# Attention with its turns two jobs behind the scores and its projections spread to the last job, and outer products that take both banks first

## The chip, the cores and the metric

One core of a Trainium2 chip runs the whole kernel. The metric is the device time in microseconds of one execution; the time of the kernel before is the median of three runs. Five engines work side by side: PE (TensorE, matmuls), DVE (VectorE), ACT (ScalarE), POOL (GpSimd) and SP, which issues the weight transfers. Each runs its own instructions strictly in order, and they meet through semaphores.

## The reference, cut to what matters

Three residual blocks follow each other on a sequence of 512 tokens with 1024 features. The first mixes gated linear attention (GLA), a convolution and a spatial gating unit, then a feed-forward network. The second has two layers, each a half feed-forward network, an attention, and another half. The third mixes a linear recurrence (LRU) and an attention. The parts that the change touches:

```python
# second block, each layer: 8 "fox" heads and 4 "diff" heads of two parts, causal, S = 512
s_f = q_f @ k_f.T * scale + cum_q - cum_k          # fox, masked, softmax, then @ v_f
a_d = softmax(s_d[0]) - lam * softmax(s_d[1])      # diff, then @ v_d, then an rms norm
out = concat(o_f, o_d) @ w_out
# third block: 8 heads of 64; with 512 tokens and blocks of 256 all past keys are selected,
# so the kernel computes plain causal attention
y = concat(lru(xl) * silu(gl), attention(q, k, v) * silu(ga)) @ w_out
# first block, GLA in chunks of 64 tokens, forward and backward
s = decay * s + k_chunk.T @ v_chunk                # the outer product of a chunk
```

## The kernel before

Everything is fp32. A projection is computed as three matmuls per pair of 128x128 tiles (the weights and the activations are each split into a high and a low part): `products`, lines 1173 to 1175. The high parts of the weights are cast on ACT (`L1551`), the low parts subtracted on POOL (`L2615`). A projection tile of 1024 inputs is thus 24 matmuls of 512 columns; the attention takes it in two half units of 12 (`T_part`). A tile of `out` with 512 inputs is 12 matmuls.

The program is one Python text that every engine walks in the same order; each engine issues only its own instructions. The order of the text is therefore the order of every engine's queue. A semaphore wait is put in only where it isn't implied already.

`attend` (line 698) interleaves the attention with other work. `at.jobs` is a list of jobs (head, query block `qt` from 0 to 3); a job has `128 * (qt + 1)` keys. In the second block's layers jobs 0 to 15 are the four diff heads and jobs 16 to 31 the four pairs of fox heads; in the third block jobs 0 to 15 are four pairs of heads. A job goes through four steps:

- `scores`: PE multiplies two parts into two banks (`L1461`) and adds the mask (`L1464`); DVE takes the maximum of each (`L2470`, `L2472`); ACT takes the exponential and its sum, with a read of the accumulator (`L1842`), which frees the bank.
- `weigh`: DVE divides by the sum (`L2482`, `L2486`, `L2488`).
- `turn`: PE transposes the weights in blocks of 128 (`L1474`); ACT copies the result to SBUF (`L1849`). The ring for these copies has two slots: a diff job uses one, a pair of heads two.
- `gather`: PE multiplies with the values (`L1488`), and frees the slots. After `qt == 3`, `head_out` takes the head to its place.

Beside these, the generator `beside` is advanced: each `next` issues one unit. In a layer the units are 8 half units of `dqk`, 16 of `fqk` (each tile ends in `fox_in` on DVE, `L2461` and `L2462`), one empty yield, two of `diff_parts` (four high parts on ACT, `L1618`, and low parts on DVE, `L2014`), and 8 tiles of `out` with an empty yield behind each. With every unit one step of `norms` for the finished diff heads goes along (root `L1589`, `L2073`; row `L1247`, `L1604`; scaling `L2518`, `L2520`). In the third block the units are 12 half units of `z` (with the rms norm of the heads: mean matmuls `L1513`, square root `L1919`, reciprocals `L2574`; and the LRU's scans `L2567`), 8 of `gl`, two with the silus and the LRU's output, one of `head_parts`, and 8 tiles of `out3`.

Written out for the third block, one iteration of the loop before is: weigh j-1, scores j, gather j-2, unit, turn j-1, unit. For the layers' jobs 16 to 31 it is: weigh j-1, scores j, gather j-5, unit, turn j-3, unit, since the loop enters from the longer lag of the diff jobs.

PSUM has 8 banks in one ring (`Slots`): a bank is taken in order of age, and taking one makes the engine wait until its last use is over. The output of the gathers holds one, an unfinished half unit another.

The GLA chain (`chain`, `outer`, lines 1362 and 1383) makes, for each of 4 heads and 7 chunk steps, one outer product forward and one backward. Each is a matmul with 64 rows; the two use different halves of the rows. Each takes a bank (and waits for it) right before its matmul.

Of the kernel before, what the change touches and what calls it, by code (L numbers as in the profile page):

```python
# [77 lines left out]
class Tally:  # L78


    def __init__(self):
        self.at, self.counting = ({}, True)
# [214 lines left out]
def ring(k, name, aps, since=()):  # L297
    if name not in k.rings:
        k.rings[name] = Slots(aps, since)
    return k.rings[name]  # L300
# [356 lines left out]
class Heads:  # L657


    def __init__(self, k, tag, order, P, since):  # L660
        self.k, self.tag, self.since = (k, tag, since)
        self.jobs = [(h, qt) for h in order for qt in range(4)]
        self.P, self.T = (ring(k, 'P ' + tag, P, since), ring(k, 'T ' + tag, k.tmp[0:2], since))
        self.N = ring(k, 'N ' + tag, k.tmp[3:], since) if tag != 'm' else None
        first = 1 if tag == 'm' else 0
        self.stats = ring(k, 'stats ' + tag, [k.sm[:, 8 * i:8 * i + 8] for i in range(first, first + 8)], since)
        self.out = 0

    def parts(self, h):

# [27 lines left out]
def attend(on, at, beside):  # L698

    scored = weighed = turned = gathered = 0  # L700
    total = len(at.jobs)
    pair = lambda j: at.jobs[j][0][0] != 'd'
    while gathered < total:
        if scored < total and pair(scored):
            if weighed < scored:
                on.weigh(at, *at.jobs[weighed])
                weighed += 1
            on.scores(at, *at.jobs[scored])
            scored += 1
        elif scored < total:  # L710
            on.scores(at, *at.jobs[scored])
            scored += 1
        if turned > gathered and (pair(gathered) or turned - gathered > 1 or scored == weighed == turned):
            h, qt = at.jobs[gathered]
            on.gather(at, h, qt)
            gathered += 1
            if qt == 3:
                on.head_out(at, h)
                at.out += 1
        if weighed < scored and (scored == total or scored - weighed > 1):  # L720
            on.weigh(at, *at.jobs[weighed])
            weighed += 1
        two = turned < total and pair(turned)
        if two:
            next(beside, None)
        if weighed > turned and (two or weighed - turned > 2 or scored == weighed):
            on.turn(at, *at.jobs[turned])
            turned += 1
        next(beside, None)
    for _ in beside:  # L730
        pass


def second(on, k, layer, before):
# [31 lines left out]
    at = Heads(k, L, [('d', i) for i in range(4)] + [('f', i) for i in range(4)], k.P2, [last, ('lambda', L), ('forgot', L)])  # L766
# [5 lines left out]
    def projections():  # L772

        turn = None
        for n in (2, 6, 3, 7):
            on.T_part(('dqk', L, n), 'dqk' + L, n, A, 0, 2)
            if turn is not None:
                on.rope(L, turn)
            yield
            on.T_part(('dqk', L, n), 'dqk' + L, n, A, 1, 2)  # L780
            on.diff_in(L, n, R, last)
            turn = n
            yield
        for n in (0, 4, 1, 5, 2, 6, 3, 7):
            on.T_part(('fqk', L, n), 'fqk' + L, n, A, 0, 2)
            if n == 0:
                on.rope(L, turn)
            yield
            on.T_part(('fqk', L, n), 'fqk' + L, n, A, 1, 2)
            on.fox_in(L, n, R, last)  # L790
            yield
        yield
        for i in range(4):
            on.diff_parts(at, i)
            if i % 2:
                yield
        for n in range(KT):
            on.T(('outd_' + L, n), 'out' + L, n, at.OA, kt=4, first=4)
            on.part(res, n, ('outd_' + L, n))
            yield  # L800
            yield

    def norms():
# [8 lines left out]
    def both():  # L812
        one, two = (projections(), norms())
        while next(one, 'end') != 'end':
            next(two, None)
            yield
    attend(on, at, both())
    for n in range(KT):
        on.T(('out2_' + L, n), 'out' + L, n, at.OA, kt=4)
# [14 lines left out]
def third(on, k, res):  # L834
# [46 lines left out]
    def projections():  # L881
# [42 lines left out]
        for n in range(KT):  # L924
            on.T(('outl', n), 'out3', n, at.OA, kt=4)
            on.part(out, n, ('outl', n))
            yield
        on.head_parts(at, 2)
    attend(on, at, projections())
    on.head_parts(at, 3)  # L930
    for n in range(KT):
# [189 lines left out]
class Tensor(Engine):  # L1121
# [225 lines left out]
    def chain_begin(self, h):  # L1347
        for v in range(2):
            self.take(self.k.banks, 'bo', h, v, hold=True)
        for d in range(2):  # L1350
            self.outer(h, 0, d)

    def intra(self, h):
        k, e = (self.k, self.e)
# [6 lines left out]

    def chain(self, h, step):
        k, e = (self.k, self.e)
        for d in range(2 if step < 6 else 0):
            self.outer(h, step + 1, d)
        for d in range(2):
            c = step if d == 0 else 7 - step
            at = slice(64 * c, 64 * c + 64)
            if step == 0:
                state = k.SIN[:, d, h, :]  # L1370
                self.wait_ge('copied state', d, h)
            else:
                state = gla_ring(k).of(('st', h, d))[:, 256 * ((step - 1) % 2):256 * ((step - 1) % 2) + 256]
                self.wait_ge('state', h, d, step - 1)
            for v in range(2):
                m = e.matmul(self.bank('bo', h, v)[:, at], state[:, v * 128:v * 128 + 128], k.QE[:, d, at], start=step == 0 and d == 0, stop=step == 7 and d == 1, skip_group_check=True)  # L1376
            m.then_inc(*k.filled.inc(('inter', h, d, step), *([('free', ('st', h, d))] if step == 7 else []), *([('filled', ('bo', h))] if step == 7 and d == 1 else [])))
# [2 lines left out]
        for v in range(2):  # L1380
            self.k.banks.let(('bo', h, v))

    def outer(self, h, step, d):
        k, e = (self.k, self.e)
        c = step if d == 0 else 7 - step
        p, w = (64 * (c % 2), 256 * (h % 2))
        b = self.take(k.banks, 'kv', h, step, d)
        self.wait_ge('kd', h, d)
        self.wait_ge('value', h // 2, c // 2)
        e.matmul(b[:, 0:256], k.KD[p:p + 64, d, c // 2, :], k.VT[p:p + 64, c // 2, w:w + 256], start=True, stop=True).then_inc(*k.filled.inc(('filled', ('kv', h, step, d))))  # L1390

    def head_scale(self, s, h):
        sq = head_sum(self.k, h)
# [570 lines left out]
def gla_ring(k):  # L1964
    return ring(k, 'gla', k.tmp, [('normed', 'nx', 7)])
# [822 lines left out]
```

## Time and profile before

| | us |
|---|---|
| median of three runs | 3550.41 (3546.18 to 3551.94) |
| the profiled execution | 3547.52 |
| its span, first to last instruction | 3545.5 |
| PE busy | 3452.7 (97%) |
| DVE, ACT, POOL busy | 1244.3, 1260.8, 1522.3 |
| mean granted clock of PE | 0.988 of full speed |

The busy time of PE counts matmuls whose ends are modelled and overlap, so the table says that PE is hardly ever idle, not that it is at its peak. A wait of PE shows as idle time before an instruction with the engine that released it. Three stretches hold the attentions: 1702.8 to 1878.5 and 2709.5 to 2885 (the two layers) and 3375 to 3520 (third block). The GLA chain runs from 200 to 401.

### The profile page before, as it was taken

Reading aid. Unit: us, or ns where it says so; the run is one execution under the profiler, and the core shown is the slowest. Engines: PE = TensorE matmul, PEld = TensorE weight load, DVE = VectorE, ACT = ScalarE, POOL = GpSimd, SP = SyncE. Lnnn points to the kernel's source line nnn. Section 1 sums busy time; section 2 is a strip of 40 time slices with the busy share of each in tenths; the row PEclk is TensorE's granted clock in tenths of the full one; section 3 lists DMA queues with packets and bytes.
Section 4 is the critical chain, followed back from the end, with each engine's and each line's share of the span. In section 5 each row is a group of like instructions: output and inputs, shape, how many; then the busy total and the mean of one; then the engine's idle time right before and its main releaser. Section 6 shows DMA issues by size and latency. Waiting matters only on the chain.

```text
span 3545.5 us, 39140 instructions
## 1 busy us (share of the span) xinstructions
PE 3452.7 (97%) x16100; PEld 2776.8 (78%) x16100; DVE 1244.3 (35%) x2103; ACT 1260.8 (36%) x1926; POOL 1522.3 (43%) x709
## 2 busy tenths in 40 slices
PE   7999999998999999999999999999999999999988
PEld 3777887887888888887777888888887778887766
DVE  3165684531221135211553111111114652111574
ACT  4433323432322332223454222322233543222464
POOL 2422344655444444445424444444445234444333
PEclk8999999999999999999999999999999999999999
DMA  6211132442233323433112233232332022233211
GB/s 231 95 54 54 60 119 99 163 148 83 107 131 126 100 89 131 146 94 105 60 33 92 96 98 92 92 105 95 92 95 92 28 75 96 100 90 107 72 42 60
DMA packets 98717, 341.17 MB, mean 96 GB/s; under 512 B 11307, under 2 KB 11563, under 8 KB 98124
## 3 DMA queue, kind: packets, MB, share of 16 engines
q1 hardware_dynamic: 97632, 334.02, 28.3%
q10 hardware_dynamic: 908, 4.67, 0.3%
q8 instruction: 127, 2.08, 0.2%
q14 instruction: 50, 0.41, 0.0%
HBM read 336.02 MB, written 2.10 MB: 95 GB/s over the span
## 4 chain that ended last, share of the span: by engine, by line
PE 90%; DVE 4%; ACT 3%; POOL 1%; issue 1%; DMA 1%; ACTq 0%; DVEq 0%
PE ps L1173 25%; PE ps L1175 25%; PE ps L1174 25%; PE ps L1192 2%; PE ps L1461 2%; PE ps L1193 2%; PE ps L1194 2%; PE ps L1488 1%; PE ps L1474 1%; PE ps L1376 1%; DVE t L2574 1%; POOL t L2615 1%; PE ps L1247 1%; DVE t L2111 1%; PE ps L1229 0%
## 5 line engine op out<-in xcount | busy, mean ns | idle before, releaser
L2615 POOL TENSOR_TENSOR t<-t,t 128x1024 fp32r<-128x1024 f32 (+2 forms) x588 | 1362.8, 2320 | 1796.5 <-ACT t L1551 1795.4
L1173 PE MATMUL ps<-t,t 128*128 128x512 f32 (+1 forms) x4048 | 1607.5, 397 | 21.9 <-POOL t L2615 13.2
L1175 PE MATMUL ps<-t,t 128*128 128x512 f32 (+1 forms) x4048 | 1584.7, 391 | 0.0
L1174 PE MATMUL ps<-t,t 128*128 128x512 f32 (+1 forms) x4048 | 1580.4, 390 | 0.0
L1173 PEld LDWEIGHTS ps<-t,t 128*128 128x128 f32 x4048 | 764.5, 189 | 188.8 <-issue 16.7
L1175 PEld LDWEIGHTS ps<-t,t 128*128 128x128 f32 x4048 | 763.5, 189 | 167.7
L1174 PEld LDWEIGHTS ps<-t,t 128*128 128x128 f32 x4048 | 764.2, 189 | 157.7 <-issue 1.0
L1551 ACT CAST t<-t 128x1024 fp32r<-128x1024 f32 (+2 forms) x588 | 584.1, 995 | 568.4 <-PE ps L1175 423.6
L2414 DVE TENSOR_TENSOR t<-t,ps 128x512 f32<-128x512 f32 x110 | 75.7, 688 | 532.2 <-PE ps L1175 516.4
L1618 ACT CAST t<-t 128x512 fp32r<-128x512 f32 x158 | 97.0, 621 | 403.5 <-DVE t L2414 359.0
L1805 ACT ACTIVATE t<-t 128x512 f32<-128x512 f32 x88 | 55.6, 632 | 318.0 <-DVE t L2407 318.0
L2014 DVE TENSOR_TENSOR t<-t,t 128x512 fp32r<-128x512 f32 x138 | 119.9, 873 | 119.8 <-ACT t L1618 119.8
L2249 DVE SCALAR_TENSOR_TENSOR ps<-t,t,ps 128x392 f32<-128x392 f32 (+14 forms) x232 | 159.0, 685 | 6.2
L2375 DVE TENSOR_TENSOR t<-ps,t 128x512 f32<-128x512 f32 x32 | 22.1, 692 | 392.5 <-PE ps L1175 392.5
L2407 DVE TENSOR_TENSOR t<-ps,t 128x512 f32<-128x512 f32 x88 | 60.7, 690 | 250.9 <-PE ps L1175 225.0
L1192 PE MATMUL ps<-t,t 128*128 128x512 f32 x336 | 138.2, 411 | 10.6 <-POOL t L2615 7.6
L1842 ACT ACTIVATE t<-ps,t 128x128 f32<-128x128 f32 (+3 forms) x160 | 83.8, 528 | 165.8 <-DVE t L2472 99.5
L1194 PE MATMUL ps<-t,t 128*128 128x512 f32 x336 | 134.1, 399 | 0.0
L1193 PE MATMUL ps<-t,t 128*128 128x512 f32 x336 | 133.9, 399 | 0.0
L2629 POOL TENSOR_TENSOR t<-t,t 128x512 f32<-128x512 f32 x41 | 55.1, 1344 | 129.9 <-ACT t L1582 105.8
L2470 DVE TENSOR_REDUCE t<-ps 128x1 f32<-128x128 f32 (+3 forms) x160 | 77.5, 485 | 57.3 <-PE ps L1464 56.2
L1787 ACT ACTIVATE t<-t,t 128x512 fp32r<-128x512 f32 x48 | 34.7, 723 | 156.3 <-DVE t L2377 107.5
(278 smaller groups left out, 2374.9 us busy)
## 6 DMA issues: line engine op xcount, KB each, us to landing
t<-in_w_f1i SPq DMA_DIRECT2D x88, 512.0 KB, 3.3
t<-in_w_f2i SPq DMA_DIRECT2D x88, 512.0 KB, 3.2
t<-in_w_ada SPq DMA_DIRECT2D x72, 512.0 KB, 4.2
t<-in_w_ffi SPq DMA_DIRECT2D x44, 512.0 KB, 3.6
t<-in_w_f1o SPq DMA_DIRECT2D x32, 512.0 KB, 3.5
t<-in_w_f2o SPq DMA_DIRECT2D x32, 512.0 KB, 3.5
t<-in_w_gate SPq DMA_DIRECT2D x24, 512.0 KB, 4.0
t<-in_w_out SPq DMA_DIRECT2D x48, 256.0 KB, 2.6
```

The lines of the kernel that those rows point to most:

```text
L1173: e.matmul(out, wh[:, at], X.hi[c][:, 0:N], start=c == first, stop=False)
L1174: e.matmul(out, wh[:, at], X.lo[c][:, 0:N], start=False, stop=False)
L1175: m = e.matmul(out, wl[:, at], X.hi[c][:, 0:N], start=False, stop=c == final)
L1192: e.matmul(out, X.hi[c][:, at], wh[:, w], start=c == 0, stop=False)
L1193: e.matmul(out, X.hi[c][:, at], wl[:, w], start=False, stop=False)
L1194: m = e.matmul(out, X.lo[c][:, at], wh[:, w], start=False, stop=c == 7)
L1551: e.copy(k.WH[:, n % NHL, 0:w], k.raw[:, j % NRAW, 0:w]).then_inc(*k.rounded.inc(('rounded', j)))
L1618: e.copy(A.hi[t], src).then_inc(*k.act.inc(('hi', A.tag, t)))
L1842: e.activation(p[:, 0:n], self.bank('s', *key)[:, 0:n], ACT.Exp, scale=0.125, bias=st[:, 1:2], accum_out=st[:, 2:3]).then_inc(*k.act.inc(( ...
L2014: e.tensor_tensor(A.lo[t], src, f(A.hi[t]), ALU.subtract).then_inc(*k.dve.inc(('lo', A.tag, t), *events))
L2249: e.scalar_tensor_tensor((c3 if j == 30 else a3)[:, :, lo:hi], h3[:, :, lo + w - 15:hi + w - 15], param(k, 'conv_w', w * 8 + i), a3[:, :, ...
L2615: e.tensor_tensor(k.WL[:, n % NHL, 0:w], k.raw[:, j % NRAW, 0:w], f(k.WH[:, n % NHL, 0:w]), ALU.subtract).then_inc(*k.rest.inc(('rest', j) ...
```

## The change

`attend` is rewritten. `two` now follows the job to be scored, not the one to be turned. In that mode a job is turned when a further one has been weighed behind it (two behind its scores), every job that is turned is gathered in the next iteration, and the number of units per iteration is a rate: 1.0 in the layers, 1.9 in the third block, 2.0 once all is scored. The empty yield behind each tile of `out` goes. In the GLA chain `outers` takes both banks, with all waits, and then issues both matmuls.

```diff
-        self.out = 0
+        self.out, self.rate = (0, 1.9 if tag == 'm' else 1.0)
...
-    total = len(at.jobs)
+    total, due = (len(at.jobs), 0.0)
     pair = lambda j: at.jobs[j][0][0] != 'd'
     while gathered < total:
-        if scored < total and pair(scored):
-            if weighed < scored:
-                on.weigh(at, *at.jobs[weighed])
-                weighed += 1
+        two = scored == total or pair(scored)
+        if two and weighed < scored:
+            on.weigh(at, *at.jobs[weighed])
+            weighed += 1
+        if scored < total:
             on.scores(at, *at.jobs[scored])
             scored += 1
-        elif scored < total:
-            on.scores(at, *at.jobs[scored])
-            scored += 1
-        if turned > gathered and (pair(gathered) or turned - gathered > 1 or scored == weighed == turned):
+        ready = turned if two else turned - 1
+        while gathered < ready:
             h, qt = at.jobs[gathered]
             on.gather(at, h, qt)
             gathered += 1
...
-        if weighed < scored and (scored == total or scored - weighed > 1):
+        if not two and scored - weighed > 1:
             on.weigh(at, *at.jobs[weighed])
             weighed += 1
-        two = turned < total and pair(turned)
         if two:
-            next(beside, None)
-        if weighed > turned and (two or weighed - turned > 2 or scored == weighed):
+            due += at.rate if scored < total else 2.0
+            if due >= 1.0:
+                due -= 1.0
+                next(beside, None)
+        while turned < weighed - (2 if not two else 1 if scored < total else 0):
             on.turn(at, *at.jobs[turned])
             turned += 1
-        next(beside, None)
+        while due >= 1.0 or not two:
+            due -= 1.0 if two else 0.0
+            next(beside, None)
+            if not two:
+                break
...
             on.T(('outd_' + L, n), 'out' + L, n, at.OA, kt=4, first=4)
             on.part(res, n, ('outd_' + L, n))
             yield
-            yield
...
-        for d in range(2):
-            self.outer(h, 0, d)
+        self.outers(h, 0)
...
-        for d in range(2 if step < 6 else 0):
-            self.outer(h, step + 1, d)
+        if step < 6:
+            self.outers(h, step + 1)
...
-    def outer(self, h, step, d):
...
+    def outers(self, h, step):
+        k, e, w = (self.k, self.e, 256 * (h % 2))
+        both = []
+        for d in range(2):
+            c = step if d == 0 else 7 - step
+            both.append((d, c, self.take(k.banks, 'kv', h, step, d)))
+            self.wait_ge('kd', h, d)
+            self.wait_ge('value', h // 2, c // 2)
+        for d, c, b in both:
+            p = 64 * (c % 2)
+            e.matmul(b[:, 0:256], k.KD[p:p + 64, d, c // 2, :], k.VT[p:p + 64, c // 2, w:w + 256], start=True, stop=True)...
```

## Rows read from the trace of the kernel before

**Rows 1.** The page's part 4: the chain of waits, by engine.
```profile
PE 90%; DVE 4%; ACT 3%; POOL 1%; issue 1%; DMA 1%; ACTq 0%; DVEq 0%
```

**Rows 2.** Waits of PE, whole span: line, releaser, us in total, times, longest.
```profile
PE ps L1488 <- ACT t L1849: 11.3, 7, 5.1
PE ps L1474 <- DVE t L2488: 8.6, 4, 3.7
```

**Rows 3.** Windows: length, busy of PE, PEld, DVE, ACT, POOL, clock, DMA share, GB/s.
```profile
1702.80:1878.50 175.70, 171.13 (x1010) 129.08 (x1010) 107.68 (x323) 89.31 (x229) 47.65 (x28) 1.00 0.12 40
...
3375.00:3520.00 145.00, 127.03 (x686) 91.21 (x684) 92.74 (x177) 82.17 (x172) 45.13 (x25) 0.95 0.13 42
```

**Rows 4.** Windows of PE alone, third block: length, PE busy, clock, DMA share, GB/s.
```profile
3405.00:3410.00 5.00, 2.62 (x12) 1.00 0.14 58
3410.00:3417.00 7.00, 5.66 (x17) 0.51 0.01 4
...
3478.30:3485.00 6.70, 5.62 (x22) 0.50 0.00 0
```

**Rows 5.** Timeline of PE, first layer: start, us, instruction, idle before and releaser.
```profile
1815.90 1.13 PE L1247 MATMUL ps<-t,t 128*128 128x128 f32 x8 [0.22 <-DVE t L2482]
...
1819.03 1.53 PE L1461 MATMUL ps<-t,t 80*128 80x384 f32 x4 [1.34 <-ACT t L1842]
...
1825.36 0.47 PE L1173 MATMUL ps<-t,t 128*128 128x512 f32 x1 [0.44 <-DVE t L2014]
...
1870.46 1.09 PE L1488 MATMUL ps<-t,t 128*64 128x128 f32 x16 [0.90 <-ACT t L1849]
...
1877.26 1.09 PE L1488 MATMUL ps<-t,t 128*64 128x128 f32 x16 [1.25 <-ACT t L1849]
```

**Rows 6.** Timeline of PE, third block.
```profile
3383.88 0.70 PE L1461 MATMUL ps<-t 64*128 64x256 f32 x4 [2.40 <-DVE t L2584]
...
3390.29 0.44 PE L1474 MATMUL ps<-t,t 128*128 128x128 f32 x2 [2.66 <-DVE t L2488]
...
3411.34 1.54 PE L1474 MATMUL ps<-t,t 128*128 128x128 f32 x6 [3.73 <-DVE t L2488]
...
3478.46 1.12 PE L1488 MATMUL ps<-t,t 128*64 128x128 f32 x8 [5.07 <-ACT t L1849]
...
3519.01 1.09 PE L1488 MATMUL ps<-t,t 128*64 128x128 f32 x16 [1.15 <-ACT t L1849]
```

**Rows 7.** Timeline of ACT and DVE, first layer.
```profile
1815.25 0.27 ACT L1589 ACTIVATE t<-ps,t 128x8 f32<-128x8 f32 x1
...
1829.62 0.69 ACT L1842 ACTIVATE t<-ps,t 128x512 f32<-128x512 f32 x1 [2.55 <-DVE t L2472]
...
1817.38 0.67 DVE L2461 TENSOR_TENSOR t<-ps,t 64x512 f32<-64x512 f32 x1
...
1819.85 0.75 DVE L2518 SCALAR_TENSOR_TENSOR t<-t,t,t 128x512 f32<-128x512 f32 x1 [1.07 <-ACT t L1604]
...
1828.65 0.69 DVE L2470 TENSOR_REDUCE t<-ps 128x1 f32<-128x512 f32 x1
...
1831.69 0.48 DVE L2488 TENSOR_SCALAR t<-t,t 128x512 f32<-128x512 f32 x1
```

**Rows 8.** Timeline of ACT and DVE, third block.
```profile
3400.62 1.28 ACT L1919 ACT_TABLE_LOAD   x1
3401.91 1.26 ACT L1919 ACTIVATE t<-ps,t 128x512 f32<-128x512 f32 x2
3403.07 0.65 ACT L1849 COPY t<-ps 128x256 f32<-128x256 f32 x2
...
3412.11 0.69 ACT L1842 ACTIVATE t<-ps,t 128x512 f32<-128x512 f32 x1 [6.61 <-DVE t L2472]
...
3402.63 6.57 DVE L2574 RECIPROCAL t<-t 128x512 f32<-128x512 f32 x2 [3.68 <-ACT t L1919]
```

**Rows 9.** Timeline of PE, the later of two outer products that a wait parts.
```profile
264.98 0.70 PE L1390 MATMUL ps<-t,t 64*128 64x256 f32 x2 [1.15 <-DVE t L2218]
```

More of the change, by code:

```diff
@@ L1381, in chain_end @@
             self.k.banks.let(('bo', h, v))
-    def outer(self, h, step, d):
[L1384 to L1390, printed above, removed]
+    def outers(self, h, step):
[8 more added lines that the diff above has]
+            p = 64 * (c % 2)
+            e.matmul(b[:, 0:256], k.KD[p:p + 64, d, c // 2, :], k.VT[p:p + 64, c // 2, w:w + 256], start=True, stop=True).then_inc(*k.filled.inc(('filled', ('kv', h, step, d))))
     def head_scale(self, s, h):
```

## The prediction

> **What bounds the kernel now.** PE is busy 97% of the span by the table, and holds 90% of the chain of waits [rows 1]. The waits of PE come next: all of them are some 93 us (span less PE busy), and those at the attention's lines are small: 11.3 us of products with the values waiting for ACT's copies, 8.6 us of transposes waiting for the weighing on DVE [rows 2]. The windows then show where: the attention of a layer takes 175.7 us (the second 175.5) with 4.6 us of idle PE at full clock, that of the third block 145 us with 18 idle and a mean clock of 0.95 [rows 3]. So order alone can win some 27 us. The question is which wait ends last at each place, and what the clock does: in the third block it was at 1.2 GHz from 3410 to 3417 and from 3478 to 3485 (0.51 and 0.50), each time following an idle PE (3.73 and 5.07 us); after waits of 2.40 and 2.66 us it stayed at 2.4 [rows 4, 6].
>
> **The order before and after**, from the loop. A job is a pair of heads and one block of queries (128 to 512 keys in turn); a half unit is 12 matmuls of a projection, 2.9 us (12 of them in 2.62 us of a window [rows 4]). In the steady state of the third block an iteration j was: scores j, gather j-2, half unit, turn j-1, half unit. It becomes: scores j, gather j-3, half unit, turn j-2, mostly a half unit. In the layers' second half (jobs 16 to 31) the old order trailed further (gather j-5, turn j-3) and used two half units per iteration until the projections were gone; the new one is scores j, gather j-3, one half unit, turn j-2. Jobs 0 to 15 of the layers keep their order.
>
> **Layers: what goes.** The old waits near the end of the fqk projections are 0.22, 1.34, 0.44 and once more some 0.4 us, and in the tail 0.90 and 1.25 [rows 5]: 4.5 us, and 5.9 with what the starts of matmuls lie further apart there (1.4 us, read from the starts). The tail gets half units: turn 31 has one behind it, and its gather (1.25) is free. But jobs 29 and 30 are now turned and gathered in a row. The ring T has two slots, a pair takes both, so ACT copies job 30 only behind gather 29: 0.86 for two copies of 384 keys (an estimate; 0.65 for 256, 1.07 for 512, by the row of 256 [rows 8]) and 0.45 of hand-over, 1.3 us of wait. The tail thus falls from 3.0 to 1.3.
>
> **Layers: what comes.** (a) Turn j-2 is now followed at once by scores j+1 and its gather, where a half unit used to lie between. With 256 keys turned and 128 scored that is 1.1 us of PE against 1.33 (two copies 0.65 [rows 8] and the hand-over): 0.25 once or twice, the other sizes fit. (b) The norm of a diff head puts a root on ACT ahead of those copies: table 1.28 and root 0.27 [rows 7]. Heads 2 and 3 meet it now, turn 15 and turn 19: 1.55 + 0.54 or 1.07 of copies + 0.3 against 1.9 and 2.4 us of PE, 0.6 each, 1.2 in all. This replaces the 1.34 and the 0.22 above. (c) The largest: three yields hold no matmul (one empty, two of diff_parts). Before, two came in one iteration; now each takes an iteration, so PE meets four scores without a half unit, right behind the last fox_in. From its end, in DVE's order: fox_in 1.36 and the last norm step 1.1 to 2.5; weighing job 23 1.1 to 3.6; the maxima of job 24 0.85 to 4.45; ACT's two exponentials with their reads to 5.1, then the copies of job 22 (0.86) to 5.95 [rows 7], the sizes below 512 keys from the same stretch. PE has done turn 21, scores 24, gather 21, turn 22 and scores 25 by 3.4 and waits 2.6. The same walk gives 1.0 for job 23, 1.35 for job 24 (behind four high parts of 0.56 each on ACT, while their four low parts of 0.65 hold DVE) and 0.9 for job 25: 5.9 in all. Bounds: 1.5 us (DVE's own work of 10.9 us in those iterations against PE's 9.7, each summed from its instructions) and 9 us, if the clock falls once. I take 5.9, since every term has a row. Per layer 0.3 + 1.2 + 5.9 + 1.3 = 8.7 against 5.9: +2.8, for both +5.6.
>
> The Trainium skill (ScalarE: Activation LUTs, What ACT_TABLE_LOAD costs) adds 1.38 us of drain to a load of 1.28, 2.66 a switch; the rows show the activation right behind a load of 1.28 (3400.62 and 3401.91) [rows 8]. By its figure (an estimate) the two places of (b) would cost 1.4 us more each, +5.5 us over both layers; the sum goes by the row.
>
> **Third block.** (d) Iteration 0 has one half unit, not two (1.9 owed). Scores 1 need a bank of the value projection, which DVE empties just before 3383.88 whatever PE does; PE waited 2.40 for it and now, one half unit earlier at it, 5.2 [rows 6]. The half unit lies behind the scores and fills the 2.66 us of turn 0: the two cancel to +0.1. But a wait of 5.2 is as long as the one after which the clock was at half; half the 5.4 us that follow is 2.7, of which I count 2.3. (e) The head norms put two 128x512 reciprocals of 3.3 us on DVE, three times (6.57 each time) [rows 8]. Before, turn 2 and turn 6 waited for the weighing behind them (3.73 [rows 6], 1.28), the second set hid. Turn 2 is one iteration later and free. But the reciprocals now come as the second half unit of iterations 2, 4 and 6, so the maxima, the exponentials of the next job and, behind these in ACT's order, the copies of the job before all queue behind them. From the end of the mean matmuls: reciprocals to 7.7 (sqrt behind a cast and a table load), weighing 1.0, maxima of 512 keys 1.6, second exponential 0.9 later, a copy of a projection 0.6, copies 0.65: 12.8. PE until gather 1: scores 1.28, gather 0.37, half unit, turn 0.36, half unit, scores 0.64: 8.5. Gather 1 waits 4.3 (perhaps as scores 4, whose bank the exponential holds); gather 3 has smaller jobs, 10.8 against 9.4, 1.4; gather 5 3.7. Sum 9.4 against 5.0. The first is again followed by a low clock with a good chance (2.5 before, 2.0 counted now). Bounds for (e): -5.0 and -2.5 of clock if the copies do not queue, +10 if each wait costs clock. (f) ACT's four silus and a table load stand ahead of the copies for gather 9 (5.07 before [rows 6], 8.4 us from the last gl half unit to the gather). Job 11 has 512 keys where job 10 had 384, 0.9 later, with 0.6 less of PE before it: 6.6. Turn 10 no longer waits 0.92. +0.6. (g) In iteration 9 turn 7 has nothing behind it, 0.3. Tail: gather 14 behind gather 13 on one ring 1.3, gather 15 1.3, for 0.77 and 1.15 before [rows 6]: +0.7. Sum (d) to (g): 0.1 + 2.3 + 4.4 - 0.5 + 0.6 + 1.0 = +7.9.
>
> **Outer products.** Both waits now stand ahead of both matmuls. The Trainium skill (TensorEngine Tiling (Array Packing), Key Properties) says tiles on different rows run in parallel, which speaks for keeping them together; but only 3 of the 28 pairs are apart (as the one whose later matmul waits 1.15 for the state update) [rows 9]. In these the second starts when its bank is free either way, and the first (0.6) moves from before the wait to beside it: 0. Bounds -1.9 (three first matmuls on the path) and +1.9.
>
> **Sum.** +5.6 + 7.9 = +13.5 on the profiled 3547.5 gives 3561. That execution lies 2.9 below the median of the three runs (3546.2 to 3551.9); against the median it would be 3564. I take 3562. What a measurement of this kernel tells from no change is 0.2%, 7.1 us: faster is below 3543.3, slower above 3557.5.
>
> **Rivals.**
> A, faster (0.15): the copies keep up. One mechanism: with turns two behind, weighing never stops PE in the third block (2.66 + 3.73 + 1.28, 2.5 of clock), gathers 1, 3 and 5 find their copies made, and the tails win 1.7 twice. That is -10.2 - 3.4 = -13.6, 3537. For it: the 8.6 us of transposes are DVE's alone. Against: ACT runs in order, and its exponential waited 6.61 us for the maxima behind the reciprocals [rows 8]. It decides at 8.5 us from the mean matmuls to gather 1: if job 1's copies come sooner, A holds.
> B, no change (0.27): the old turn waits and new gather waits are of one size, and (c) is at its lower bound since PE's own work covers DVE: about +2, 3552.
> C, the clock (0.16): each of the new waits of 3 us and more (scores 1, gathers 1 and 5, the two layers' gather 22) is followed by a spell at 1.2 GHz that costs 2.5 to 3.4. Beyond what is counted that is 3 more, +9: 3571. Rows 4 speak for it, since both long waits had one; against it, the waits of 2.4 and 2.66 had none.
> The forecast's own case holds 0.42 (3554 to 3570). Slower over 0.2% is C and nearly all of it, 0.58; within 0.2% B and little else, 0.28; faster 0.14. The range takes in most of B and the near end of A, and reaches above C: 3542 to 3578.
>
> **What would show it.** In the changed profile: the 8.6 us of transposes waiting for the weighing nearly gone, and waits of gathers for copies up from 11.3 to over 25 us in all; scores 1 of the third block waiting over 5 us; after the last fqk unit three gathers or scores in a row that wait; gather 1 waiting over 3 us right behind the reciprocals; three or four spells at half clock in the third block instead of two; the tail with one wait of 1.3 per layer; the outer products' stretch unchanged within 2 us. I am wrong if gather 1 doesn't wait, or if the stretch of either layer comes out below 175 us.

## The result, and the profile after

The changed kernel takes 3559.55 us (median of 13 runs, 3555.91 to 3568.3) against 3550.37 of the kernel before in the same session (13 runs): ratio 1.0029 [1.0022, 1.0037]. That is 9.2 us slower by the medians and 8 to 13 by the interval. The prediction was 3562. The profiled execution took 3560.8 (span 3558.9), 13.3 more than that of before.

The windows of the profile after, stretch by stretch: the two layers' attention from first scores to last gather, the third block's, and the stretch of the outer products. Columns as in [rows 3].

```profile
1701.80:1882.90 181.10, 175.09 (x1009) 131.99 (x1008) 108.56 (x323) 90.57 (x228) 46.79 (x28) 0.97 0.11 37
2714.20:2894.10 179.90, 172.26 (x1010) 130.42 (x1009) 109.19 (x323) 90.25 (x228) 46.77 (x28) 0.99 0.12 38
3385.90:3533.40 147.50, 127.56 (x685) 92.31 (x684) 90.10 (x177) 81.80 (x171) 42.98 (x25) 0.93 0.13 42
...
199.10:404.20 205.10, 196.66 (x1107) 159.01 (x1106) 121.16 (x217) 67.53 (x89) 51.34 (x23) 0.97 0.15 52
```

The first layer's and the outer products' stretch in the kernel before, cut at the same points:

```profile
1702.80:1878.30 175.50, 170.93 (x1010) 128.88 (x1009) 107.68 (x323) 89.21 (x228) 47.65 (x28) 1.00 0.12 40
...
200.40:400.40 200.00, 195.31 (x1105) 156.52 (x1104) 121.15 (x217) 67.43 (x89) 51.47 (x23) 0.98 0.16 52
```

So the layers are longer by 5.6 and 4.4 us, the third block by 2.7 (144.8 before), the outer products by 5.1. The rest of the program gives 4.5 back in this pair of executions (4.8 between the outer products and the first layer, at places the diff doesn't touch). Idle PE is length less busy: 4.6 before in a layer, 6.0 and 7.6 after. The rest of the layers' loss is PE being busy longer at a lower clock (175.1 and 172.3 against 170.9). In the first layer most of it is one spell at half clock that begins in the wait of gather 22 (PE alone; length, busy, clock, DMA share, GB/s):

```profile
1832.20:1842.40 10.20, 9.64 (x46) 0.50 0.00 0
```

The waits of PE over the whole span after, answering to [rows 2] (L1495 gathers, L1856 ACT's copies, L1468 scores, L2591 DVE's copies of the value projection, L2489 the weighing, L1849 the exponentials, L1397 outer products, L2225 the state update):

```profile
PE ps L1495 <- ACT t L1856: 22.4, 16, 6.1
...
PE ps L1397 <- DVE t L2225: 5.5, 3, 1.9
...
PE ps L1468 <- DVE t L2591: 5.1, 1, 5.1
...
PE ps L1468 <- DVE t L2489: 2.9, 1, 2.9
...
PE ps L1468 <- ACT t L1849: 2.7, 4, 1.6
```

The 8.6 us of transposes waiting for the weighing are gone, as meant. Gathers went from 11.3 to 22.4, and scores from 5.1 (2.4 and 2.7 before) to 10.7 (5.1, 2.9 and 2.7). The timeline of PE shows where: the second layer first, then the third block.

```profile
2798.26 2.50 PE L1495 MATMUL ps<-t,t 128*128 128x128 f32 x10 [1.25 <-ACT t L1856]
2823.56 0.88 PE L1495 MATMUL ps<-t,t 128*64 128x128 f32 x12 [0.67 <-ACT t L1856]
2846.72 0.88 PE L1495 MATMUL ps<-t,t 128*64 128x128 f32 x12 [2.42 <-ACT t L1856]
2854.61 0.44 PE L1495 MATMUL ps<-t,t 128*64 128x128 f32 x4 [1.12 <-ACT t L1856]
2859.46 0.66 PE L1495 MATMUL ps<-t,t 128*64 128x128 f32 x8 [0.44 <-ACT t L1856]
2885.63 0.88 PE L1495 MATMUL ps<-t,t 128*64 128x128 f32 x12 [1.05 <-ACT t L1856]
...
3394.55 1.22 PE L1468 MATMUL ps<-t 64*128 64x256 f32 x4 [5.08 <-DVE t L2591]
3422.25 0.49 PE L1468 MATMUL ps<-t 64*128 64x128 f32 x4 [2.91 <-DVE t L2489]
3443.76 1.09 PE L1495 MATMUL ps<-t,t 128*64 128x128 f32 x16 [0.83 <-ACT t L1856]
3461.90 0.49 PE L1468 MATMUL ps<-t 64*128 64x128 f32 x4 [1.61 <-ACT t L1849]
3463.70 1.12 PE L1495 MATMUL ps<-t,t 128*64 128x128 f32 x8 [1.10 <-ACT t L1856]
3494.76 1.12 PE L1495 MATMUL ps<-t,t 128*64 128x128 f32 x8 [6.07 <-ACT t L1856]
3526.83 0.88 PE L1495 MATMUL ps<-t,t 128*64 128x128 f32 x12 [1.05 <-ACT t L1856]
3532.40 1.09 PE L1495 MATMUL ps<-t,t 128*64 128x128 f32 x16 [0.87 <-ACT t L1856]
```

In order these are gathers 13, 18, 22, 24, 25 and 30 of a layer, then scores 1, scores 4, gather 3, scores 8, gather 5, gather 9, and the two gathers of the tail. The first of them is the one that the prediction has no term for. ACT's timeline ahead of it shows what stands before the copies (2797.84): the exponentials of job 16, a copy, a cast and a square.

```profile
2795.19 0.37 ACT L1849 ACTIVATE t<-ps,t 128x128 f32<-128x128 f32 x1 [5.71 <-PE ps L1481]
...
2795.89 0.58 ACT L1864 COPY t<-ps 128x512 f32<-128x512 f32 x1
2796.36 1.06 ACT L1558 CAST t<-t 128x1024 fp32r<-128x1024 f32 x1
2797.30 0.64 ACT L1878 ACTIVATE t<-t 128x512 f32<-128x512 f32 x1
2797.84 0.76 ACT L1856 COPY t<-ps 128x256 f32<-128x256 f32 x2
```

### The profile page after: what moved, and what is told of

Its sections match the earlier page's. It is cut to its first block, busy times and chain, and to the rows that moved or that the text cites. A ratio compares the mean times of both kernels' runs of the same rounds, so it can differ in the third digit from the quotient of the medians.

```text
span 3558.9 us, 39103 instructions
## 1 busy us (share of the span) xinstructions
PE 3461.6 (97%) x16100; PEld 2786.9 (78%) x16100; DVE 1241.0 (35%) x2103; ACT 1263.0 (35%) x1926; POOL 1520.7 (43%) x709
## 4 chain that ended last, share of the span: by engine, by line
PE 91%; DVE 3%; ACT 3%; POOL 1%; issue 1%; DMA 1%; ACTq 0%; DVEq 0%
PE ps L1177 26%; PE ps L1179 25%; PE ps L1178 25%; PE ps L1196 2%; PE ps L1197 2%; PE ps L1198 2%; PE ps L1468 2%; PE ps L1495 1%; PE ps L1379 1%; PE ps L1481 1%; DVE t L2581 1%; PE ps L1251 1%; POOL t L2622 1%; DVE t L2118 1%; PE ps L1397 0%
## 5 line engine op out<-in xcount | busy, mean ns | idle before, releaser
L1177 PE MATMUL ps<-t,t 128*128 128x512 f32 (+1 forms) x4048 | 1610.0, 398 | 18.3 <-POOL t L2622 11.3
L1849 ACT ACTIVATE t<-ps,t 128x128 f32<-128x128 f32 (+3 forms) x160 | 84.3, 529 | 154.2 <-DVE t L2479 122.4
L2066 DVE SCALAR_TENSOR_TENSOR t<-t,t,t 128x1024 f32<-128x1024 f32 x49 | 80.9, 1651 | 33.6 <-DMA t<-in_w_ada 33.5
```

The costliest lines, as they stand in the source:

```text
L1177: e.matmul(out, wh[:, at], X.hi[c][:, 0:N], start=c == first, stop=False)
L1849: e.activation(p[:, 0:n], self.bank('s', *key)[:, 0:n], ACT.Exp, scale=0.125, bias=st[:, 1:2], accum_out=st[:, 2:3]).then_inc(*k.act.inc(( ...
```

## The experiments: the parts of the change

**One: the outer products alone**, in the kernel before.

```diff
-        for d in range(2):
-            self.outer(h, 0, d)
+        self.outers(h, 0)
```

> Only the outer products are changed; both attentions keep the order of before. My theory (the waits only move from between two matmuls to ahead of them): the stretch from the first to the last outer product stays 200 us but for spells of the lower clock, the three separated pairs show one wait of 1.8 us ahead of both instead of 1.1 between them, attentions at 175.4, 175.4 and 144.8, total within 2 us of before. Rival (the pairs gain by running side by side): 2 us less in that stretch. Rival (the state updates get late, which explains the 205 us seen with the whole change): 3 to 5 us more, in every run.

3547.44 us, ratio 0.9999 [0.9990, 1.0008] (3 rounds). The stretch took 200.3 against 200.0. The three separated pairs wait 1.86 us ahead of both matmuls, where before a matmul, a wait of 1.15 and the second matmul stood: the ends are the same. In this pair of profiles the edit costs 0.3 us.

**Two: the new loop in the layers alone; three: in the third block alone.** Both keep the new outer products; the other stage uses the old loop.

```diff
+def attend(on, at, beside):
+    (attend_new if at.tag != 'm' else attend_old)(on, at, beside)
```

> The new loop only in the two layers of the second block, the old one in the third block, outer products new. Theory: the layers carry most of the loss, since ACT's copies now stand between a turn and the gather two steps behind it: attention stretches of 180 to 181 and 180 us, 144.8 in the third block, total +8 to +10 against before. Rival (the loss is made in the third block, by scores 1 and the gathers behind the reciprocals): total within 3 us of before.

3551.67 us, 1.0009 [1.0001, 1.0018]. The layers took 179.4 and 179.3 us, the third block 144.5.

```profile
1702.30:1881.70 179.40, 172.17 (x1009) 130.36 (x1008) 109.32 (x323) 90.50 (x229) 46.84 (x28) 0.99 0.12 38
```

Idle PE is 7.2 us (4.6 before), busy PE 1.2 more: +3.9 per layer, of which 2.7 are waits and the rest goes with 3.4 us at half clock from gather 22 on. The two layers are thus 7.7 us longer in this profile, near what was expected, but the total moved by 3.2 (0.4 to 6.4) and not by 8 to 10; why the rest doesn't reach the total stays open.

> The new loop only in the third block, the old one in the layers, outer products new. Theory: turn waits are exchanged for gather waits of nearly the same size; stretch 147 to 148 us against 144.8, layers 175.4 each, total +2 to +4. Rival (what the prediction gave): +7.9 in that stretch.

3552.18 us, 1.0009 [1.0000, 1.0018]. Third stretch 148.1 (+3.3), with the same waits as in the changed kernel. The stretch is what the theory said, 147 to 148. The two parts alone sum to 6.4 us, the whole measures 9 to 10; with intervals of some 3 us on each part, the difference can't be called an interaction.

**Four: turns before the half unit**, that is, the changed kernel without the half unit between gathers and turns.

```diff
             due += at.rate if scored < total else 2.0
-            if due >= 1.0:
-                due -= 1.0
-                next(beside, None)
         while turned < weighed - (2 if not two else 1 if scored < total else 0):
```

> As the changed kernel, but the turn comes right behind the gather and all units behind the turn: a half unit then lies between a turn and the next gather, and ACT makes the copies ahead of the unit's casts and high parts. Theory (copies behind ACT's queue are what PE waits for in the layers): gather 13 no longer waits 1.25, nor gathers 15 and 18 to 21; gather 22 still waits about 2.4 as its copies stand behind an exponential that DVE holds up; layers at 176.5 to 178 us each, 3 to 4 less than with the change. In the third block the wait for the silus moves from gather 9 to the first tile of out3, 146 to 148. Total 6 to 8 us below the changed kernel. Rival (the loss comes from the lack of units in four iterations alone): layers still 179 or more.

3559.02 us, 1.0027 [1.0017, 1.0036]: no better than the change. The wait of gather 13 is gone, but those of gathers 22, 24 and 25 grew from 2.42, 0.85 and 0.46 (first layer of experiment two) to these, in the first layer:

```profile
1837.79 1.47 PE L1492 MATMUL ps<-t,t 128*64 128x128 f32 x12 [3.03 <-ACT t L1853]
1847.33 0.44 PE L1492 MATMUL ps<-t,t 128*64 128x128 f32 x4 [1.39 <-ACT t L1853]
1852.95 0.66 PE L1492 MATMUL ps<-t,t 128*64 128x128 f32 x8 [1.27 <-ACT t L1853]
```

A layer came to 178.9 and 179.0, 0.3 to 0.5 under experiment two and not the expected 176.5 to 178: the rival held. The third block came to 144.7, 2.8 under the changed kernel (gather 9 waits 1.55, the first tile of `out3` 3.8 for POOL), but the outer products' stretch was 206.8 in this profile. In the layers, what PE doesn't wait at one place it waits at the next that depends on the same queue.

## The experiments: what the waits hang on

**Five: half units spread.** The splits of the diff heads ride on fox half units, so that one empty iteration remains behind the last of these and one is put four later.

```diff
+            if n == 3:
+                on.diff_parts(at, 0)
+            if n == 7:
+                on.diff_parts(at, 1)
             yield
...
+            if n == 7:
+                on.diff_parts(at, 2)
             yield
+        on.diff_parts(at, 3)
         yield
-        for i in range(4):
-            on.diff_parts(at, i)
-            if i % 2:
-                yield
...
             yield
+            if n == 3:
+                yield
```

> The changed kernel, but the splits of the diff heads' tiles ride on half units of the last fox projections (head 0 with fqk 3, heads 1 and 2 with fqk 7), so that of the three yields without matmuls one is left for head 3, and one empty yield is put between the fourth and fifth tile of the output projection. The four scores in a row without a half unit become two single iterations, four apart. My theory (term c): the waits of that zone, 2.4, 0.2, 1.1 and 0.4 in the second layer, are owed to the missing half units in a row: they fall to 1.5 or less, each layer's stretch from 180 to 181 to 177 to 178, the total by 4 to 7. Rival (DVE's own work sets that zone, its 10.9 us against PE's 9.7): half of it stays wherever the half units lie; the stretch falls by 1 to 1.5 only. Second rival: the splits on ACT and DVE now stand ahead of the exponentials of jobs 20 and 22 and make waits of their own there; 180 stays.

3563.01 us, 1.0039 [1.0026, 1.0053]; layers 181.6 and 180.8. My theory fell for the first wait and held for those behind it: gathers 24 and 25 no longer wait, but gathers 18 and 22 (the two rows) wait 1.19 for 0.67 and 3.54 for 2.42, and gather 31 of the tail waits 0.87 where it was free. Idle PE is 8.5 us a layer, 1.3 more.

```profile
2826.33 0.88 PE L1500 MATMUL ps<-t,t 128*64 128x128 f32 x12 [1.19 <-ACT t L1861]
2850.59 0.88 PE L1500 MATMUL ps<-t,t 128*64 128x128 f32 x12 [3.54 <-ACT t L1861]
```

DVE's timeline tells why. Behind the last fox_in (L2473, L2474) now stands a low part of the split (L2026, 0.69), then the norm (L2530 and one more), the weighing, and only then the maxima for which ACT's exponential waits, with a high part of the split (0.61 on ACT) and the copies for gather 22 behind it:

```profile
2844.25 0.69 DVE L2474 TENSOR_TENSOR t<-ps,t 64x512 f32<-64x512 f32 x1
2844.98 0.69 DVE L2026 TENSOR_TENSOR t<-t,t 128x512 fp32r<-128x512 f32 x1
2845.59 0.75 DVE L2530 SCALAR_TENSOR_TENSOR t<-t,t,t 128x512 f32<-128x512 f32 x1
...
2847.81 0.29 DVE L2482 TENSOR_REDUCE t<-ps 128x1 f32<-128x128 f32 x1
```

0.69 + 0.61 = 1.3 us more in the queues, 1.1 more of wait. The walk of term (c) through the queues is thus right; that it needs four iterations without a half unit is not. The first wait hangs on what stands in DVE's queue behind the last half unit.

**Six and seven: no reciprocals.** The head norms' reciprocals of the third block work on 8 of 512 columns, in the changed kernel and in the kernel before (the rest of that norm is left out).

```diff
-            e.reciprocal(m, m).then_inc(*k.dve.inc(('head rstd', n)))
+            e.reciprocal(m[:, 0:8], m[:, 0:8]).then_inc(*k.dve.inc(('head rstd', n)))
```

> The changed kernel with the head norms' reciprocals on 8 of 512 columns only (the norms of the third block's queries and keys are thus left out for the others). My theory (term e): the two reciprocals of 3.3 us in a row are what scores 4 (2.9 us), gather 3 (0.8), scores 8 and gather 5 (1.6 and 1.1) wait for, through the maxima and the exponentials queued behind them. All of these go, and the spells at 1.2 GHz from 3423 to 3426 and 3464 with them: the third stretch falls from 147.5 to 137 to 140. Scores 1 keeps its 5 and gather 9 its 6. Rival (ACT's own load in those iterations, with two table loads): scores 4 and gather 5 still wait over 1.5 each, and the stretch stays above 142.

> The kernel before with the head norms' reciprocals on 8 of 512 columns only, as in the leave-out run of the changed kernel (the norms of the third block's queries and keys are left out for the others). It tells what the new order is worth when DVE is not behind. My theory: of the old waits turn 0 (2.66) and scores 1 (2.40) and gather 9 (5.1) stay, turn 2 (3.7), its spell (3.4 lost) and turn 6 (1.3) go: third stretch 144.8 to 136 to 137.5, above the changed kernel's 134.6 in the same leave-out, so that the order itself gains 1.5 to 3 there and it is the place of the reciprocals that turns this into a loss. Rival: the old order gains as much or more without them (134.6 or less), so that the new order loses by itself, through scores 1 and gather 9.

One execution of each, 3546.80 and 3541.53 us; third stretches, the changed order first:

```profile
3384.60:3519.20 134.60, 124.06 (x685) 89.92 (x685) 65.47 (x175) 79.89 (x167) 42.01 (x25) 0.96 0.14 46
```

```profile
3379.80:3514.00 134.20, 123.74 (x685) 89.37 (x684) 73.70 (x175) 79.75 (x167) 43.83 (x25) 0.97 0.14 46
```

Scores 4 and 8 and gathers 3 and 5 no longer wait; even scores 1 fall to 2.5, which I had expected to keep their 5 (in the changed kernel DVE's two reciprocals at 3369.54 stand ahead of the value copies, too). The rival, ACT's own load, fell with the waits. So the reciprocals cost 12.9 us in the new order and 10.6 in the old, and the difference, 2.3, is nearly the whole of the third block's 2.7, as far as one execution of each can tell. But my view that the new order gains 1.5 to 3 by itself fell: without reciprocals both take the same within 0.4. It is neither better nor worse there, it only takes the reciprocals at a worse place.

**Eight: two half units in iteration 0** of the third block, in the changed kernel.

```diff
-    total, due = (len(at.jobs), 0.0)
+    total, due = (len(at.jobs), 0.1 if at.tag == 'm' else 0.0)
```

> The changed kernel, but the third block starts with 0.1 owed, so that iteration 0 has both half units and iteration 1 one. My theory (term d): scores 1 wait for a bank that DVE empties at a fixed time; with one more half unit in front the wait falls from 5.1 to 2.3 as it was before, the spell at 1.2 GHz from 3392 (6.8 us, worth 3.4) no longer follows, and since turn 0 stays one iteration later, the 2.7 us that it cost before don't come back: third stretch 147.5 to 142 to 144.5, total 3 to 5 less. Rival: what PE saves at scores 1 it waits at scores 4, whose bank comes with the exponentials behind the reciprocals at a time of its own: 2.9 there becomes 5 to 6, and the stretch stays at 146 to 147.5.

3561.07 us, 1.0040 [1.0026, 1.0054]; third stretch 150.2, 2.7 longer where 3 to 5.5 less was expected. Scores 1 wait 2.40 again, and what follows waits instead:

```profile
3398.68 0.70 PE L1468 MATMUL ps<-t 64*128 64x256 f32 x4 [2.40 <-DVE t L2591]
3408.00 0.47 PE L1177 MATMUL ps<-t,t 128*128 128x512 f32 x1 [1.52 <-POOL t L2622]
3413.57 3.33 PE L1520 MATMUL ps<-t,t 128*128 128x512 f32 x4 [2.57 <-ACT t L1922]
3427.66 0.80 PE L1468 MATMUL ps<-t 64*128 64x128 f32 x4 [2.69 <-DVE t L2489]
```

The rival had this at scores 4; it is the mean matmuls (L1520) that wait, for ACT's squares. The 2.7 us saved at scores 1 came back as 4.1 (1.52 and 2.57) in other places than either theory named, and PE was busy 1.5 us longer.

## The experiments: can it be had faster

**Nine: heads split early.** In the kernel before, a pair's query norm comes one iteration ahead of its key norm, so that no two reciprocals follow each other.

```diff
-                    on.head(pair, half + 1)
                     on.head(pair + 4, half + 1)
...
             on.head_in(n, last)
+            on.head(n, 0)
             yield
...
                 on.T_part(('z', n + 4), 'z3', 12 + n, A, half, 2)
+                on.head(n, half + 1)
...
-            on.head(n, 0)
```

> The kernel before, but the query half of each pair's head norm (mean matmul, root, reciprocal, scaling) comes one iteration earlier than the key half, so that the reciprocals of 3.3 us stand alone instead of two in a row. My theory: it is the 6.6 us in a row that turn 2 (3.7 us, and the spell at 1.2 GHz after it) and turn 6 (1.3) wait for; with 3.3 at a time the slack of an iteration covers them: the third stretch falls from 144.8 to 137 to 140, the total by 5 to 8 below the kernel before. Rival: each root now has a table load of 1.28 and one back to the exponentials of its own on ACT, three pairs more; the copies and exponentials come later by 2.6 in each iteration and PE waits 1 to 1.5 at each of three more places: 142 to 146, total within 3 of before.

3550.24 us, 1.0007 [0.9998, 1.0016]; third stretch 149.9, 5 longer. The rival held, and more: the mean matmuls wait 2.70 for a square just issued, and ACT is busy 90.4 us in the stretch, 8 more, and gathers wait for its copies, up to 1.89.

**Ten: key reciprocals late.** Means, roots and table load stay together; only the second reciprocal and its scaling are issued one iteration later on DVE. **Eleven:** the same on the changed kernel.

```diff
-                    on.head(pair + 4, half + 1)
+                    on.head(pair + 4, 3 * half + 1)
...
+                if half == 0 and pair is not None:
+                    on.head(pair + 4, 3)
+                    on.head(pair + 4, 2)
...
-        if s == 1:
+        if s == (1 if n in (0, 1, 2, 3, 4) else 3):
```

> The kernel before, but in the third block the reciprocal of a pair's keys and its scaling are issued one iteration later than those of its queries; mean matmuls, roots and their table load stay together. Between the two reciprocals of 3.3 us now lie the weighing and the maxima of an iteration. My theory: turn 2 (3.7 us and the spell at 1.2 GHz behind it) and turn 6 (1.3) wait for two reciprocals in a row; with one of 3.3 the slack covers it, and there is no second table load as in the earlier split: the third stretch falls from 144.8 to 136 to 140, the total by 5 to 8. Rival: the scores of the next pair need the scaled keys, and DVE, which is now behind, is late with them: scores 4 wait 2 to 4 us instead, the stretch stays at 143 to 146.

> The same edit on the changed kernel. My theory: scores 4 (2.9) wait for a bank held by an exponential behind both reciprocals, as do scores 8 and gather 5 (1.6 and 1.1); with one reciprocal at a time these fall by 3.3 each to nothing, as far as the leave-out run showed (134.6): third stretch 147.5 to 138 to 142, scores 1 and gather 9 keep their 5 and 6; the total 6 to 9 below the changed kernel, 3550 to 3554, still above the kernel before with this edit by what scores 1, the layers and gather 9 cost. Rival: in this order a pair's scores follow the last half unit of its norm more closely (in iteration 4 only one half unit lies between), so scores 4 wait for the scaled keys: 145 to 147.

On the kernel before: 3546.36 us, 0.9994 [0.9985, 1.0003], third stretch 140.6, 4.3 shorter, between the theory's 136 to 140 and the rival's 143 to 146. On the changed one: 3556.93, 1.0032 [1.0021, 1.0044], third stretch 145.2, 2.3 shorter, as the rival had it; the total shows none of it. Turn 2 no longer waits 3.73, turn 6 not 1.28; scores 4 wait, as the rival said:

```profile
3418.28 0.49 PE L1466 MATMUL ps<-t 64*128 64x128 f32 x4 [2.74 <-DVE t L2566]
```

and on the changed kernel

```profile
3418.72 0.80 PE L1473 MATMUL ps<-t 64*128 64x128 f32 x4 [4.12 <-DVE t L2494]
```

(2.91 before this edit). In both, PE starts 0.15 us after DVE has scaled the pair's keys (the ends of that are 3418.13 and 3418.56); the rows name the instruction behind it. Scores 8, gathers 3 and 5 are free in both.

**Twelve: gates first.** As ten, with the gl projections ahead of those of the last pair, so that the silus ride on a half unit.

```diff
+        on.T_part(('z', 3), 'z3', 11, A, 0, 2)
         for n in range(4):
             on.lru_silu(n)
...
+        yield
```

> The kernel before with the late key reciprocals, and the gate projections (gl) put ahead of the last pair's query and key projections, so that the four silus ride on a half unit of the latter instead of standing with the splits behind the last half unit. My theory: gather 9's 5.1 us are copies queued behind four silus and their table load on ACT after the last half unit; with silus two iterations earlier, among half units, that wait falls under 2.5 and the spell at 1.2 GHz from 3478 goes: third stretch another 3 to 6 below the run with late reciprocals alone, 131 to 136 if that one is at 138. Rival: the wait follows the missing half units, not the silus: two yields without matmuls remain behind z 7 with the splits of the recurrence's tiles on ACT, and the gather there waits 4 to 5 again; only the place changes. Second rival: the silus delay the exponentials among the half units by 3.8 us and a turn there waits 2 or more instead.

3545.77 us, 0.9993 [0.9984, 1.0002]; third stretch 141.8 where 131 to 136 was expected. Gather 9's wait for copies falls from 5.07 to 2.50, and a wait of 2.00 for the split of the recurrence's tiles on POOL comes behind it, with the low clock behind both. The first rival, that the wait follows the missing half units, is borne out in part. Against ten nothing was won. Ten and twelve are the fastest measured of the kernels that leave nothing out, but neither is told from the kernel before by its interval.

## Why the prediction was right, and where it was not

The sign and the main mechanism held: turns no longer wait for the weighing, and gathers and scores wait longer for what stands in the queues of ACT and DVE. That the size held is in good part luck. In the profiles +13.3 stands against +13.5 predicted, but the layers lost 4.4 us more than forecast and the third block 5.2 less; the outer products' 5.1 and the 4.5 that the rest gave back cancel too, and neither was forecast.

Of the signs named beforehand, the 8.6 us are gone, the third block has four spells at half clock (from 3392, 3423, 3464 and 3491), scores 1 wait over 5 us, and in the second layer gathers 22 to 25 wait in a row. Others failed: gathers wait 22.4 us for copies and not over 25, the outer products' stretch is not within 2 us, and gather 1 doesn't wait, which was one of the two signs of being wrong. It is scores 4, right ahead of it, that wait, 2.91 us; behind the reciprocals they do stand.

**Layers, +2.8 each predicted.** Waits came as +2.7 in experiment two (idle 7.2 against 4.6), but as a sum of misses. Inside, (c) was 5.9 and measured 3.9 (2.42, 0.16, 0.85, 0.45); its first term of 2.6, walked from rows, measured 2.42, the later ones came out smaller. The tail was 1.3 and is 1.05: the hand-over, 0.45 in the sum without a row, is 0.2 beside the 0.86 of copies. (b), 0.6 twice behind a root and its table load, didn't come: the 0.67 at gather 18 has two exponentials, a cast and a square ahead of its copies (2822.57), and the table load only behind them (2824.63).

Missed was gather 13, 1.25: I held that jobs 0 to 15 keep their order and gave the transition nothing, but there turns 13 and 14 and then gathers 13 and 14 come in a row behind ACT's other work. And what goes was 5.9 by my count and 4.6 by idle PE; the 1.4 that I read from the starts was not to be had.

The step that failed is the clock: the forecast's own sum priced none in the layers. In the changed kernel's profile the layers' PE was busy 4.2 and 1.3 us longer, with a mean clock of 0.97 and 0.99 against 1.00. That is no accident of one execution: all ten layer stretches with the new loop (changed kernel, two, six, eight, eleven) have 3.4 to 10.2 us at half clock, nine of them from gather 22 on, and take 179.2 to 181.2 us; with the old loop 11 of 14 have none and take 175.5, three have 3.4 us of it and take 177.1. This is rival C's mechanism, at a place that C names, gather 22.

**Third block, +7.9 predicted, +2.7 in the profile, +3.3 in experiment three.** (d) 5.2 at scores 1 for 2.40, turn 0 free: 5.08, right. Its clock, 2.3, came as 2.0: from the start of scores 1 to that of the twelfth matmul of the half unit behind them it is 5.32 us (3394.55 to 3399.87), before it was 3.36 (3383.88 to 3387.24).

(e) 9.4 against 5.0 predicted: scores 4 took 2.91 for 4.3, gather 3 0.83 for 1.4, scores 8 and gather 5 together 2.71 for 3.7, and scores 6 0.42 without a term; 6.9 against 5.0, so +1.9 and not +4.4. That it is the reciprocals is shown by experiments six and seven, but each predicted length was 0.6 to 1.4 too long. The walk's pieces add up to 12.45, not to its 12.8, and DVE's rows show another piece that was wrong:

```profile
3411.84 6.57 DVE L2581 RECIPROCAL t<-t 128x512 f32<-128x512 f32 x2 [3.59 <-ACT t L1926]
...
3419.12 0.68 DVE L2477 TENSOR_REDUCE t<-ps 128x1 f32<-128x512 f32 x1
...
3420.70 1.41 DVE L2585 SCALAR_TENSOR_TENSOR t<-t,t,t 128x512 f32<-128x512 f32 x2
```

```profile
3420.03 0.69 ACT L1849 ACTIVATE t<-ps,t 128x512 f32<-128x512 f32 x1 [6.35 <-DVE t L2479]
...
3421.41 0.19 ACT L1849 ACTIVATION_READ_ACCUMULATOR t<-ps,t 128x1 f32 x1
...
3421.96 0.66 ACT L1856 COPY t<-ps 128x256 f32<-128x256 f32 x2
```

From the end of the reciprocals (3418.41) to that of the copies (3422.62) it is 4.2 us, where the walk had 5.1: the first maximum starts 0.7 behind, not 1.0, and the pieces after it lap. Nor is it a bank held by the exponential that scores 4 wait for, as (e) guessed: ACT's last read ends at 3421.60, DVE's scaling of the pair's queries and keys (L2585), which these scores read, at 3422.11, and PE starts at 3422.25.

(f) 6.6 predicted, 6.07 found, turn 10 free of its 0.92: +0.1 for +0.6. (g) 1.05 + 0.87 for 0.77 + 1.15: nothing, for +1.0. The waits sum to +2.0, busy PE makes the other 0.7. The forecast had +1.8 for the clock in (d) and (e); scores 8 have a spell that it left out, while gather 9's now falls half into the wait.

**Outer products, 0 predicted.** 0.3 by experiment one. In the profile after, the stretch is 5.1 longer; PE is busy 1.4 us more in it and idle 3.8 more (8.4 against 4.7), of which the three moved waits are 2.1 and a wait of 2.7 for DVE (1.1 before) 1.6, with a mean clock of 0.97 against 0.98. Over all profiles it took 200.0 to 201.6 us with the old form (5 executions) and 200.3 to 206.8 with the new (9), though the code up to there is one and the same within each form. The means are 2.9 apart, experiment one's interval reaches to +2.8: whether the longer wait ahead of both matmuls makes a low clock behind it more likely stays open. It may be the part that the sum of experiments two and three lacks.

Rival A fell (gathers didn't keep up). B's +2 is near the 3.2 that either part alone shows, but not the whole. C's spells came at nearly all the places it names, but cost less than its +9. The Trainium skill's drain at a table switch (ScalarE: Activation LUTs, What ACT_TABLE_LOAD costs) doesn't show here either: the root's activation starts at 3411.12, 1.30 us after the start of a load of 1.28.

## What to carry to other kernels

Turning one block later moves a wait from the engine that weighs to the one that copies; it gains only if that one's queue is not itself behind the same slow instruction. Walk both queues from the end of the last half unit to the operand needed next: that gave 2.6 for 2.42 without a run, but 4.3 for 2.91 where the reciprocals stood in them. To shorten such a wait take work out of the queue, or put the long instruction elsewhere in it (4.3 us of the stretch here for a one-place move); moving PE's own half units brought waits back elsewhere, and lowered the time in none of three experiments (four, five, eight).

## What the runs showed of the hardware that was not expected

A spell at half clock costs less when part of it falls into a wait. Around the end of the 5.08 us at scores 1 PE was at 0.57 in a window of 7.5 us, only 3.95 of them busy, and the spell cost 2.0 us; behind 2.91 and 1.10 the clock fell as well, with PE busy throughout. The last row is of experiment ten, behind the wait of 2.40 at scores 1:

```profile
3391.00:3398.50 7.50, 3.95 (x12) 0.57 0.19 67
3423.00:3426.60 3.60, 3.60 (x16) 0.56 0.02 5
3464.00:3467.60 3.60, 3.60 (x16) 0.56 0.00 0
```

```profile
3389.00:3392.40 3.40, 3.40 (x10) 0.50 0.02 5
```

So waits of 1 to 3 us, which the prediction had held harmless by [rows 6], can have it behind them: the changed kernel is at half clock behind waits of 1.61 and 1.10, while the kernel before stayed at full clock behind 2.40 and 2.66. And it differs between executions of one stretch of code: experiment ten has the spell behind that same wait of 2.40, and the layers with the old loop took 175.5 us in most profiles and 177.1 in three.
